# A two-block transformer kernel on one core: stage ends and beginnings by token tile instead of by column half

## What is computed

```
# block one, per layer (DEPTH = 2)
h = rmsnorm(x, g_pre_mix); proj = h @ w_in            # 1024 -> 3404, then four kinds of attention -> mix
x = x + rmsnorm(mix @ w_out, g_post_mix)              # stage end: norm of a product, add to x
h = rmsnorm(x, g_pre_mlp)
m = square(relu(h @ w_up)) @ w_down                   # 1024 -> 4096 -> 1024
x = x + rmsnorm(m, g_post_mlp)                        # stage end
x = x + sigmoid(x @ w_ple_gate) * (p_i @ w_ple_proj)  # stage end
# block two, per layer (DEPTH = 2)
mix = hybrid_mixer(x)                                 # x @ w_in_2 (1024 -> 11648), attention, retention, w_out
x = layer_norm(ALPHA * x + mix, ln1_g, ln1_b)         # stage end
ffn = (silu(x @ w_gate) * (x @ w_up)) @ w_down        # 1024 -> 2816 -> 1024
x = layer_norm(ALPHA * x + ffn, ln2_g, ln2_b)         # stage end
```

## Time and profile before

| what | value |
|---|---|
| median of 3 runs | 2087.35 us |
| the profiled execution's own time | 2086.5 us |
| its span in the profile | 2084.7 us |
| mean granted TensorE clock | 0.956 of full |
| PE busy | 1924.9 us, 92% of the span |
| DVE busy, ACT busy | 1165.3 us (56%), 887.3 us (43%) |
| the chain that ended last | PE 80%, DVE 7%, issue 4%, DVEq 4%, ACT 3% |

### The profile page before, as it was taken

How to read it: one execution, slowest core, us unless ns; L and a number is a source line. 1 busy time by engine, 2 the same in 40 slices (tenths; PEclk the granted TensorE clock), 3 DMA queues, 4 the chain that set the end, 5 groups by cost and what they waited for, 6 DMA issues and landing times.

```text
span 2084.7 us, 25827 instructions
## 1 busy us (share of the span) xinstructions
PE 1924.9 (92%) x9126; PEld 1586.0 (76%) x9126; DVE 1165.3 (56%) x1311; ACT 887.3 (43%) x1033; POOL 69.2 (3%) x97
## 2 busy tenths in 40 slices
PE   4988999989879999899899999998998899989996
PEld 3876888778768887787777777886787777778885
DVE  3675555557745555546466565455556466565544
ACT  3543544455434444444335433443343345434442
POOL 2210000021100000000000000000000000000000
PEclk9988999999779999999999999999999999999998
DMA  5413455544655555564355653555664355654553
GB/s 189 148 60 127 151 191 171 173 162 140 84 154 185 191 175 182 167 210 131 112 181 183 200 185 125 190 182 192 200 196 133 93 181 182 217 171 132 184 193 107
DMA packets 199789, 340.33 MB, mean 163 GB/s; under 512 B 14617, under 2 KB 64921, under 8 KB 199691
## 3 DMA queue, kind: packets, MB, share of 16 engines
q1 hardware_dynamic: 194240, 327.94, 48.1%
q0 software_dynamic: 4752, 10.76, 2.8%
q10 hardware_dynamic: 699, 0.35, 0.1%
HBM read 333.24 MB, written 5.77 MB: 163 GB/s over the span
## 4 chain that ended last, share of the span: by engine, by line
PE 80%; DVE 7%; issue 4%; DVEq 4%; ACT 3%; DMA 1%; SPq 0%; POOL 0%; POOLq 0%; ACTq 0%
PE G L574 20%; PE G L575 20%; PE G L580 19%; PE T L599 5%; PE A L574 4%; PE A L575 4%; PE A L580 4%; DVE wlo L1433 2%; ACT whi L1030 1%; ACT arena L1030 1%; PE A L652 1%; DVEq L1473 1%; PE T L642 1%; DMA raw<-in_w_mlp_up 1%; DVE SCO L1636 1%
## 5 line engine op out<-in xcount | busy, mean ns | idle before, releaser
L1433 DVE TENSOR_TENSOR wlo<-raw,whi 128x2048 fp32r<-128x2048 f32 (+3 forms) x320 | 676.4, 2116 | 671.0 <-ACT whi L1030 670.8
L1030 ACT ACTIVATE whi<-raw 128x2048 fp32r<-128x2048 f32 (+3 forms) x320 | 566.0, 1769 | 760.9 <-PE G L580 666.0
L574 PE MATMUL G<-whi,XH 128*128 128x512 f32 (+1 forms) x1600 | 640.7, 400 | 6.6 <-DVE XL L1448 6.6
L575 PE MATMUL G<-whi,XL 128*128 128x512 f32 (+1 forms) x1600 | 629.7, 394 | 0.0
L580 PE MATMUL G<-wlo,XH 128*128 128x512 f32 (+1 forms) x1600 | 393.9, 388 | 0.0
L574 PEld LDWEIGHTS G<-whi,XH 128*128 128x128 f32 x1600 | 306.5, 192 | 71.9 <-issue 6.4
L575 PEld LDWEIGHTS G<-whi,XL 128*128 128x128 f32 x1600 | 306.0, 191 | 63.0 <-issue 1.9
L580 PEld LDWEIGHTS G<-wlo,XH 128*128 128x128 f32 x1600 | 299.7, 188 | 62.0 <-DVE wlo L1433 0.9
L599 PE MATMUL T<-ident,arena 128*128 128x128 f32 x812 | 126.6, 299 | 49.3 <-ACT arena L1030 21.3
L599 PEld LDWEIGHTS T<-ident,arena 128*128 128x128 f32 x812 | 100.9, 152 | 72.4 <-ACT arena L1030 21.9
L599 PE MATMUL T<-ident,X 128*128 128x128 f32 x160 | 34.2, 382 | 75.6 <-DVE X L1959 18.5
(11 more groups left out here) (191 smaller groups left out, 1724.7 us busy)
## 6 DMA issues: line engine op xcount, KB each, us to landing
raw<-in_w_in SPq DMA_DIRECT2D x112, 1024.0 KB, 6.4
raw<-in_w_mlp_up SPq DMA_DIRECT2D x32, 1024.0 KB, 5.4
raw<-in_w_mlp_down SPq DMA_DIRECT2D x32, 1024.0 KB, 5.0
raw<-in_w_ffn_gate SPq DMA_DIRECT2D x44, 512.0 KB, 4.1
raw<-in_w_ffn_up SPq DMA_DIRECT2D x44, 512.0 KB, 5.0
raw<-in_w_ffn_down SPq DMA_DIRECT2D x44, 512.0 KB, 3.3
raw<-in_w_out SPq DMA_DIRECT2D x16, 1024.0 KB, 5.0
raw<-in_w_ret_proj SPq DMA_DIRECT2D x16, 1024.0 KB, 5.3
```

The source lines that it names most:

```text
L574: nc.tensor.matmul(dst(m), hx[:, k0 + k, rows], hi[:, k, :], start=first and k == 0, stop=False)
L575: nc.tensor.matmul(dst(m), lx[:, k0 + k, rows], hi[:, k, :], start=False, stop=False)
L1030: return nc.scalar.activation(out_, in_, func, **kw)
L1433: tt(wlo[:, c % PARTS, 0:n], raw[:, slot, 0:n], whi[:, c % PARTS, 0:n].bitcast(F32), ALU.subtract).then_inc(s_lo.sem, 1)
```

## The change

**Ends.** A new `last_columns` runs the two last units tile by tile: all 24 matmuls of tile 0 (12 from each unit, by the new `half_unit`), then `s_half`, then the 24 of tile 1. Square, gain, mean, root, invert and add (or residual and layer norm) are now done for one tile's 1024 columns, then for the other's; `s_xh` now says that tile 0 of X is complete, `s_x` that tile 1 is.

**Beginnings.** `first_chunk` waits for tile 0, transposes its 8 blocks, runs tile 0's half of both units, then waits for tile 1, transposes its blocks and runs tile 1's halves. The splits of transposed data (`row_hi`, `row_lo`) are for one tile: where the gain is folded in, an instruction is 128 wide and there are twice as many (16 instead of 8 per beginning and engine); elsewhere it stays 512 wide and their number stays. A weight unit's `s_used` now comes with tile 1's half.

**Streams.** ACT's and DVE's streams are reordered to match. PE's PLE unit writes another PSUM pair. The output is written in two transfers of 512 KB, one per tile. The number of matmuls and transposes is the same, and so is the number of table loads on ACT.

The diff, cut to its core:

```diff
+
+            def half_unit(blk, L, m, c, hx, lx, k0, kb, dst, first, last):
+
+                hi = whi[:, c % PARTS, 0:kb * COLS].rearrange("p (k n) -> p k n", n=COLS)
+                lo = wlo[:, c % PARTS, 0:kb * COLS].rearrange("p (k n) -> p k n", n=COLS)
+                rows = slice(m * P, (m + 1) * P)
+                pe.wait_ge(s_hi.sem, s_hi.at(blk, L, c + 1))
+                for k in range(kb):
+                    nc.tensor.matmul(dst(m), hx[:, k0 + k, rows], hi[:, k, :], start=first and k == 0, stop=False)
+                    nc.tensor.matmul(dst(m), lx[:, k0 + k, rows], hi[:, k, :], start=False, stop=False)
+                pe.wait_ge(s_lo.sem, s_lo.at(blk, L, c + 1))
+                for k in range(kb):
+                    mm = nc.tensor.matmul(dst(m), hx[:, k0 + k, rows], lo[:, k, :], start=False,
+                                          stop=last and k == kb - 1)
+                if m == 1:
+                    mm.then_inc(s_used.sem, 1)
+                return mm
+
+            def last_columns(blk, L, c, hx, lx, k0, kb, banks, first=False):
+
+                for m in range(TILES):
+                    for n in range(2):
+                        mm = half_unit(blk, L, m, c + n, hx, lx, k0, kb, bank_pair(banks[n]), first, True)
+                    if m == 0:
                         mm.then_inc(s_half.sem, 1)
-                mm.then_inc(s_used.sem, 1)
 ...
+            def row_turn(blk, L, t, m):
+
+                for b in range(2):
+                    transposes(blk, L, 0, t + 2 * m + b, [X[:, m, (UK * b + k) * P:(UK * b + k + 1) * P] for k in range(UK)])
+
             def first_chunk(blk, L, c, t, xh, x, group=0):
 
-
-                for k, (ready, n) in enumerate(((s_xh, xh), (s_x, x))):
-
-                    pe.wait_ge(ready.sem, ready.at(blk, L, n))
-                    turn(blk, L, 0, t + 2 * k, X[:, :, k * COLS:(k + 1) * COLS], UK)
-                for k in range(2):
-
-                    pe.wait_ge(s_tfree.sem, s_tfree.at(blk, L, t + 2 + 2 * k))
-                    unit(blk, L, 0, c + k, XH, XL, UK * k, UK, COLS, bank_pair(group), k == 0, k == 1)
+                pe.wait_ge(s_xh.sem, s_xh.at(blk, L, xh))
+                row_turn(blk, L, t, 0)
+                for m in range(TILES):
+                    for k in range(2):
+                        if (m, k) == (1, 0):
+                            pe.wait_ge(s_x.sem, s_x.at(blk, L, x))
+                            row_turn(blk, L, t, 1)
+                        pe.wait_ge(s_tfree.sem, s_tfree.at(blk, L, t + 2 * m + k + 1))
+                        half_unit(blk, L, m, c + k, XH, XL, UK * k, UK, bank_pair(group), k == 0, k == 1)
 ...
-                down(0, U_DN7, False, True, T_MLP + 16)
-
-                pe.wait_ge(s_sq.sem, s_sq.at(0, L, 6))
-                pe.wait_ge(s_ng.sem, s_ng.at(0, L, 6))
-                unit(0, L, 0, U_PLE1, YH, YL, 0, 2, COLS, bank_pair(1), True, True)
+                pe.wait_ge(s_tfree.sem, s_tfree.at(0, L, T_MLP + 16))
+                last_columns(0, L, U_DN7, MH, ML, 0, UK, (1, 2))
 
                 pe.wait_ge(s_pp.sem, s_pp.at(0, L, 1))
-                first_chunk(0, L, U_PLE1 + 1, T_PX, 2, 2)
+                unit(0, L, 0, U_PLE1, YH, YL, 0, 2, COLS, bank_pair(0), True, True)
+
+                pe.wait_ge(s_sq.sem, s_sq.at(0, L, 7))
+                pe.wait_ge(s_ng.sem, s_ng.at(0, L, 7))
+                first_chunk(0, L, U_PLE1 + 1, T_PX, 2, 2, 1)
+
                 pe.wait_ge(s_pp.sem, s_pp.at(0, L, 2))
-                chunk(0, L, 0, U_PLE1 + 3, 1)
+                for m in range(TILES):
+                    for k in range(2):
+                        mm = half_unit(0, L, m, U_PLE1 + 3 + k, XH, XL, UK * k, UK, bank_pair(0), k == 0, k == 1)
+                    if m == 0:
+                        mm.then_inc(s_half.sem, 1)
 
             with pe.Fori(0, DEPTH) as L:
 ...
-                turn_hi(0, L, 0, 0, UK, XH, gain=prec[:, 0])
                 hi(0, L, 0, 0)
-                turn_hi(0, L, 0, 2, UK, XH[:, UK:KB], gain=prec[:, 0, UK:KB])
+                row_hi(0, L, 0, 0, prec[:, 0])
                 hi(0, L, 0, 1)
+                row_hi(0, L, 0, 1, prec[:, 0])
                 act.wait_ge(s_x.sem, s_x.at(0, L, 0))
 ...
+                hi(0, L, 0, U_OUT + 3)
+                act.wait_ge(s_half.sem, s_half.at(0, L, 1))
+                square(2, 0, 0, 1)
+                square(2, 0, 1, 0)
+                root(0, L, 3, 2, 1, 0)
+                hi(0, L, 0, U_MLP)
+                act.wait_ge(s_used.sem, s_used.at(0, L, U_OUT + 3))
+                square(2, 1, 0, 1)
+                act.wait_ge(s_used.sem, s_used.at(0, L, U_OUT + 4))
+                square(2, 1, 1, 0)
+                row_hi(0, L, T_N2, 0, prec[:, 1])
+                root(0, L, 4, 2, 1, 1)
+                hi(0, L, 0, U_MLP + 1)
+                row_hi(0, L, T_N2, 1, prec[:, 1])
 ...
-                squares(4, 1, 2, U_DN7 + 2)
+                his(0, L, 0, U_DN7, U_DN7 + 1)
+                act.wait_ge(s_used.sem, s_used.at(0, L, U_PLE0 + 1))
+                act_(PP[:, :, 0:COLS], pair(0), ACT.Copy).then_inc(s_pp.sem, 1)
+                act.wait_ge(s_half.sem, s_half.at(0, L, 2))
+                square(4, 0, 0, 1)
+                square(4, 0, 1, 2)
+                root(0, L, 6, 4, 1, 0)
+                hi(0, L, 0, U_PLE1)
+                square(4, 1, 0, 1)
+                act.wait_ge(s_used.sem, s_used.at(0, L, U_DN7 + 2))
+                square(4, 1, 1, 2)
                 hi(0, L, 0, U_PLE1 + 1)
-                root(0, L, 5, 4, 2)
-
-                for n, unit in enumerate((U_PLE0, U_PLE1)):
-                    act.wait_ge(s_used.sem, s_used.at(0, L, unit + 1))
-                    act_(PP[:, :, n * COLS:(n + 1) * COLS], pair(n), ACT.Copy).then_inc(s_pp.sem, 1)
-                turn_hi(0, L, 0, T_PX, KB, XH)
-                his(0, L, 0, U_PLE1 + 2, U_PLE1 + 3, U_PLE1 + 4)
+                row_hi(0, L, T_PX, 0)
+                root(0, L, 7, 4, 1, 1)
+                act.wait_ge(s_used.sem, s_used.at(0, L, U_PLE1 + 1))
+                act_(PP[:, :, COLS:DM], pair(0), ACT.Copy).then_inc(s_pp.sem, 1)
+                hi(0, L, 0, U_PLE1 + 2)
+                row_hi(0, L, T_PX, 1)
+                his(0, L, 0, U_PLE1 + 3, U_PLE1 + 4)
                 for n in range(2):
 ...
-                his(1, L, 0, 0, 1)
-                turn_hi(1, L, 0, 0, KB, XH)
+                hi(1, L, 0, 0)
+                row_hi(1, L, 0, 0)
+                hi(1, L, 0, 1)
+                row_hi(1, L, 0, 1)
 ...
-                turn_hi(1, L, 0, T2_FX, KB, XH)
+                hi(1, L, 0, V_OUT + 3)
+                root(1, L, 5, 2, 1, 0)
+                hi(1, L, 0, V_FFN)
+                row_hi(1, L, T2_FX, 0)
+                root(1, L, 6, 2, 1, 1)
                 hi(1, L, 0, V_FFN + 1)
+                row_hi(1, L, T2_FX, 1)
 ...
```

DVE's side, the new orders alone (row_lo mirrors row_hi; row_spread and row_norm are layer_norm for one tile):

```diff
+                row_mean(2, 0)
+                invert(0, L, 3, 2, 1, 0)
+                add_normed(2, 0)
+                lo(0, L, 0, U_MLP)
                 times_gain(L, 2, 0, 1, 0, 1)
-                invert(0, L, 3, 2, 2)
-                add_normed(2)
-
-                turn_lo(0, L, 0, T_N2, KB, XH, XL, gain=prec[:, 1])
-                lo(0, L, 0, U_OUT + 5)
+                times_gain(L, 2, 0, 1, 1, 0)
+                row_mean(2, 1)
+                row_lo(0, L, T_N2, 0, prec[:, 1])
+                invert(0, L, 4, 2, 1, 1)
+                add_normed(2, 1)
+                lo(0, L, 0, U_MLP + 1)
+                row_lo(0, L, T_N2, 1, prec[:, 1])
                 dve.wait_ge(s_ss.sem, s_ss.at(0, L, 2))
                 mean(3, 2, DM).then_inc(s_ms.sem, 1)
-                invert(0, L, 4, 3, 2).then_inc(s_rs.sem, 1)
 ...
+                times_gain(L, 4, 1, 0, 1, 2)
+                row_mean(4, 0)
+                invert(0, L, 6, 4, 1, 0)
+                add_normed(4, 0)
                 lo(0, L, 0, U_PLE1)
-                invert(0, L, 5, 4, 2)
-                add_normed(4)
-
-                turn_lo(0, L, 0, T_PX, KB, XH, XL)
-                los(0, L, 0, U_PLE1 + 1, U_PLE1 + 2, U_PLE1 + 3, U_PLE1 + 4)
-                for n, done in enumerate((s_xh, s_x)):
+                times_gain(L, 4, 1, 1, 0, 1)
+                times_gain(L, 4, 1, 1, 1, 2)
+                row_mean(4, 1)
+                row_lo(0, L, T_PX, 0)
+                invert(0, L, 7, 4, 1, 1)
+                add_normed(4, 1)
+                los(0, L, 0, U_PLE1 + 1, U_PLE1 + 2)
+                row_lo(0, L, T_PX, 1)
+                los(0, L, 0, U_PLE1 + 3, U_PLE1 + 4)
+
+                def gated_add(n, m):
+
 ...
+                        ins.then_inc(s_sgf.sem, 1)
                     dve.drain()
-                    tt(X[:, :, cols], X[:, :, cols], TMP, ALU.add).then_inc(done.sem, 1)
-                    dve.drain()
+                    return tt(X[:, m, cols], X[:, m, cols], TMP[:, m], ALU.add)
+
+                gated_add(0, 0)
+                gated_add(0, 1)
+                gated_add(1, 0).then_inc(s_xh.sem, 1)
```

(59 more changed lines are left out.)

207 lines of the change are left out of this document (106 added, 101 removed).

## The result

The changed kernel takes **2100.68 us** (median of 4 runs, 2096.89 to 2101.90) against 2087.54 us for the kernel before in the same job; the ratio is **1.0064, 95% interval [1.0052, 1.0077]**: slower by 13.1 us. The forecast was +9.9 us, with a range of 2090 to 2105.

A forecast was written before the change was run, and what follows sets the result against it. PE, 80% of the chain, was taken to lose time where it stands still. Place-by-place changes summed to +8.3 us, plus 1.6 for a clock fall: +9.9, from 2087.35 to 2097.3 us, range 2090 to 2105.

The forecast's parts named there:

- First weight matmuls: Start of products at each beginning: 35.0 at program start, 207.55 at the layer 0 MLP (3.6 earlier), 402.35 at the gate.
- Ends: Tile 0's X stands before tile 1's matmuls end at the MLP, so PE's wait for it goes; FFN 1 us after.
- Second pause: Before tile 1's products, nothing covers its splits: 3.25 us from first transpose to matmul with gain, 2.05 without.
- Gate: Both gates: first gate wlo stands behind tile 1's update of X, so PE waits 2.55 us; +1.45 each in all.
- clock terms: Slow matmuls after idle: 0.7 us at each of eight restarts (5.6), plus 1.6 for one fall in a second pause.
- 3.5 more slow ones: At the restart of eight beginnings, all but the gates: 3.5 more matmuls at low clock, 0.7 us each beginning.
- one fall in four: In the four long second pauses the clock falls once, making eight matmuls 0.2 slower: 1.6 us.
- Rival 1: Same time: 128-wide pieces at their lower bound and no clock term, +0.5 us, within 0.2%; chance 0.13.
- Rival 2: Much slower: clock falls in all four long and half of six short second pauses, +19.5 us, 2107; chance 0.12.
- Rival 3: Faster: clock never falls at the first tile, each of eight beginnings loses 1.7 us of slowness, 2082; chance 0.05.

The follow-up runs named there:

- e1: Changed kernel with tile 1's wait for X and eight transposes put between tile 0's two half units instead of behind both: 2082.29 us.
- e4: Changed kernel with the w_in beginning of block one as in the kernel before, except that PE waits for both tiles of X before all transposes: 2093.51 us.
- e3t: Changed kernel with 28 to 44 extra identity transposes behind tile 0's at eight beginnings, filling PE's idle time before the first product: 2092.24 us.
- f3: Changed kernel with the pre-norm gains left out of the splits of x at block one's w_in and the MLP: 2092.43 us.

## Why the prediction was right, and where it was off

**First weight matmuls: right.** Forecast 35.0, 207.55 and 402.35. Measured 35.21; 215.26 and 409.81 less the 7.5 lost upstream are 207.7 and 402.3. The same holds for the later ones: MLP of layer 1 -6.3 for -6.2, w_in of block two -3.8 for -3.8, FFN -3.9 for -4.0 each. Reading the order of each queue and adding durations is reliable.

**Ends: right.** In block one X of tile 0 stands when the products end; at the MLP the transposes follow at 210.90 with no wait. At the FFN they wait 0.93 us (forecast 1), and at the w_in of block two, layer 1, 3.3. But most of what was won there became the wait for XL, as worked out.

**Second pause: right.** From the first transpose to the product 2.99 us with gain (225.20 - 222.21; forecast 3.25, lower bound 2.7) and 2.0 without (forecast 2.05), 1.3 us less in the sum of the ten. The waits of PE in it are 1.96 and 0.98, where the forecast named 2.4 and 1.2. The pieces of 128 columns are cheaper than I took:

```profile
214.08 2.16 DVE L1531 SCALAR_TENSOR_TENSOR XL<-T,prec,XH 128x128 fp32r<-128x128 f32 x8
```

Eight in 2.16 us, one 0.343: a pitch of 0.26, where I had taken 0.28 on DVE and 0.30 on ACT. The mechanism is shown by e1: with the transposes half a unit earlier the whole pause goes.

**Gate: right.** wlo wait 2.25 for 2.55, twice.

**The step that was off is the size of the clock terms.** "I take 3.5 more slow ones, 0.7 us, at each of the eight": from the first product to tile 1's transposes the 24 products took 6.9 to 8.5 us instead of 5.44, together 18.2 too much; before, the first 24 of the same beginnings lost 9.6. That is +8.6 where the sum had +5.6. And "one fall in four": three of the four long second pauses (start, w_in of layer 1, MLP of layer 1) were followed by slow products, 1.8 us each, 5.3 instead of 1.6. These 6.7 us explain start, w_in of layer 1, MLP of layer 1 and the last FFN in the table. Against them stand the 1.3 us of the pauses and 2.25 us in the attention of block two: a low stretch of the kernel before at 947 us (and one at 1569) has no counterpart after the change. The idle time ahead is the same. A row of PE's timeline and a stretch with its granted clock, first of the kernel before, then of the changed one:

```profile
947.56 3.01 PE L599 MATMUL T<-ident,arena 128*128 128x128 f32 x12 [1.88 <-DVE arena L1503]
...
945.00:955.00 10.00, 8.12 (x44) 0.83 0.32 112
```

```profile
963.25 0.87 PE L622 MATMUL T<-ident,arena 128*128 128x128 f32 x6 [1.87 <-DVE arena L1587]
...
959.00:970.00 11.00, 8.87 (x60) 1.00 0.46 168
```

I had not counted that such stretches come and go. 6.7 - 1.3 - 2.25 leaves 3.15 of the 4.0 us by which the traces exceed the forecast. So the total came as near as it did partly by luck, of the kind that e4 had against it; without those 2.25 us the time would be 2103, still inside the range.

**Rivals.** Rival 1 (same) needed the pieces at their lower bound and no clock term; the pieces came halfway to it, but the clock term was larger than in the forecast. Rival 2 (the clock falls in the second pauses) came in three of ten places, not in seven; its reason, that transposes count for nothing, is refuted by e3t. Rival 3 (the clock never falls at the first tile) did not come: 3.32 us of idle did not keep it.

## What to carry to other kernels

Splitting a handover by rows instead of columns paid here only once the second part's preparation stood behind work of the first part that needs it no sooner: put it one half unit earlier in the in-order stream, and 13 us of loss became 4 of gain. Look for the new wait in the queue that has just been relieved, before asking for faster producers. An engine whose clock falls when it idles can be given cheap work in the gap. Here it paid where that work started directly behind the last real work, was over before the awaited data came, and no second gap followed.

## What was not expected of the hardware

Transposes alone held the granted clock at 1.00 over 5 us (1260.1 to 1265.1 in e3t), and it rose from 0.50 to 1.00 while PE ran nothing else (1463 to 1468.7 in e3t). Eight single-tile transposes behind a full stretch, followed by 3.3 to 9.2 us of idle, did not. Idle of 0.98 us behind eight transposes never lowered it (none of 40), idle of 1.96 did in 12 of 18. And the length of a low stretch after the same idle of 4.95 us was 6.8 us at one FFN and 10.2 at the other, and 6.8 at that other one too in the second trace of the same program. Two builds that differ in one place can differ by several us elsewhere (e4), and the spread of one kernel's runs (2085.16 to 2096.10 for f3) is as wide as some effects looked for here.
